# Moving two modulation units of the first scan chunk from its end into the place behind its first level update

## The chip, the cores and the metric

The kernel runs on one core of one Trainium2 chip. The metric is the device time of one execution in microseconds (us).

## The reference

Two layers of a diffusion trunk over 512 latent tokens and 256 context tokens, model width 1024, float32. Each layer modulates its input with shifts, scales and gates that come from a conditioning vector, then runs a mixer (latent attention, a bidirectional gated delta rule, pooling) and a mixture of experts. Two parts matter here.

The modulation is a matrix product of two vectors (one for latent, one for context tokens) with a matrix of 1024 by 6144 per layer:

```python
m = jnp.split(jax.nn.silu(c) @ ada_w[l] + ada_b[l], ADA_CHUNKS, axis=-1)
mc = jnp.split(jax.nn.silu(c_ctx) @ ada_w[l] + ada_b[l], ADA_CHUNKS, axis=-1)
```

The gated delta rule is a scan over chunks of tokens. Each chunk needs the inverse of a unit lower triangular matrix, and its state depends on that of the chunk before:

```python
w = lax.linalg.triangular_solve(tmat, kb * jnp.exp(gc)[..., None], ...)
u = lax.linalg.triangular_solve(tmat, vc * bc[..., None], ...)
def step(s, inp):
    v_new = u_i - jnp.einsum('bhcd,bhde->bhce', w_i, s)
    ...
```

## The kernel before, in words

The kernel is written as one program for each engine: PE (TensorE, matrix products), ACT (ScalarE), DVE (VectorE), POOL (GpSimd) and SP (SyncE, which issues the large loads). Each program is a fixed list in order; engines wait for each other on semaphores. Products go to 8 PSUM banks, handed out in rotation by `claim`: a bank can be claimed again only after its last product was read out, and the order of all claims in the PE program settles which bank a product gets.

**The scan** takes the 768 tokens in 6 chunks (`NT`), j = 0 to 5, for both directions and 4 heads at once. Within a chunk PE inverts the triangular block by levels: for each of two levels a `level_factor` (L1145), whose result DVE reads into `gW` (L2923), and a `level_update` (L1163), whose four results ACT copies back into the block (L2339). The next level's factor needs these copies. Then come the last level's product (`z6`, L1257), read out by ACT (L2344), and `u6` (L1269). A chunk has seven slots, 0 to 6, filled by `gdn_between`: slot 0 at its start, 1 behind the first factor, 2 behind the first update, 3 behind the second factor, 4 behind the second update, 5 behind z6, 6 behind u6. The table `BETWEEN` puts the state products of chunk j-1 into slots 0 to 3 and those that prepare chunk j+1 into slots 4 to 6. In chunk 0 slots 0 to 3 hold no state products. ACT's program has the same slots. In slots 3 and 5 of chunk 0 it also computes the decays of chunk 1 for one direction each (`next_decays`, L2209 to L2217), and there they stand behind the slot's modulation units. POOL multiplies these decays (`decays`, L3418), then copies the inverse of the chunk (L3534, L3535), and with that releases the first product of the next chunk (`v`, L1076) on PE.

**The modulation units.** The 48 column blocks of 256 columns of the modulation matrices are numbered; 0 to 7 are used at the start of the kernel, and from block `ADA_FIRST` = 8 on they are spread over the slots of the first layer's scan, 6 in a chunk, in the order of their numbers, as the table `ADA_SLOTS` says (its first row for chunk 0, its second for all others). One unit consists of:

- a load of 1 MB (`in_ada_w`) by SP (L1786) into one of 4 buffers of `ring`, `LENT` of them; SP issues these loads in order, each as soon as the last use of its buffer is done. Units 8 to 13 use buffers 3, 0, 1, 2, 3, 0. Buffer 2 holds tables of the scan at first, so the load of unit 11 also waits for POOL's `one_sided(0)` (L3427);
- 16 products on PE (`ada_load`, L717) into a claimed bank;
- on ACT (`ada_out`) a copy of the bank to one of two row buffers `arow` (L1940, profile name dT) and two small DMAs of 4 KB that write the rows to memory (L1949, `ada_rows`). As there are two row buffers, the copy of unit a first waits until the writes of unit a-2 have landed:

```python
if ADA_FIRST <= a - 2 < ADA_LATE:
    act.wait_ge(*ada_written(a - 2))
m = act.copy(arow[:, a % 2, :], b[:, 0:SLOT_COLS])
```

The write itself waits for the copy on the same engine, and everything behind it in ACT's list waits with it. The rows are read back at the end of the scan.

Of the kernel before, what the change touches and what calls it, by code (L numbers as in the profile page):

```python
# [92 lines left out]
    (("kr", 0), ("kr", 1), ("kk", 0)), (("ks", 0), ("ks", 1)), (("kk", 1), ("t0", 0), ("qk", 0), ("qk", 1)))  # L93
G_SLOTS = (3, 5)
GATES, SUMS, ROWS, LANES_EXP = (2, 1), (6, 3), (8, 4), (11, 7)
ADA_SLOTS = ((0, 1, 0, 1, 1, 1, 2), (1, 1, 1, 1, 1, 1, 0))


ADA_LOADS = 6 * D // 256
# [70 lines left out]
def build_program(nc, A, out):  # L170
    ctx = ExitStack()
    with ctx:
# [368 lines left out]
        def ada_at(j, slot):  # L541

            counts = ADA_SLOTS[min(j, 1)]
            first = ADA_FIRST + ADA_CHUNK * j + sum(counts[:slot])
# [3147 lines left out]
```

How the kernel before makes its waits and increments, by code:

```python
        def in_sum_made(eng, l, name, q):  # L305
            eng.wait_ge(sems[l]["lin"], sums_of(l) + 4 * q + int(name[1]))
# [1 line left out]
        def tokens_made(eng, l):  # L309
            eng.wait_ge(sems[l]["comb"], l * (1 + IN_PAIRS) + 1)
# [1 line left out]
        def taps_added(eng, l, q):  # L313
            eng.wait_ge(sems[l]["comb"], l * (1 + IN_PAIRS) + 2 + q)
# [5 lines left out]
        def lead_copied(eng, l, n):  # L321
            eng.wait_ge(sems[l]["lead"], l * (IN_PAIRS + OUT_PAIRS) + n + 1)
# [1 line left out]
        def sum_made(eng, l, name, p=0):  # L325
            eng.wait_ge(sems[l]["lin"], sums_of(l) + 4 * IN_PAIRS + OUT_SUMS[l].index((name, p)) + 1)
# [168 lines left out]
        def product_ready(eng, key, i=None):  # L496
            b, n, per = where[key]
            eng.wait_ge(bank_full[b], plus(n + 1, per, i))
            return psum[:, b, :]
# [5 lines left out]
        def evacuated(eng, key, i=None):  # L506
            b, n, per = where[key]
            eng.wait_ge(bank_free[b], plus(n + 1, per, i))
# [100 lines left out]
            def bank_unused(b):  # L610
                if b in second_of:
                    pe.wait_ge(bank_free[second_of[b][0]], second_of[b][1])
                elif uses[b]:
                    pe.wait_ge(bank_free[b], uses[b])
# [39 lines left out]
            def weights(name, n=None):  # L655
# [8 lines left out]
                        slot = len(loads) % (LENT if lends else SLOTS)  # L664
                    n = take_slot(name, slot)
                pe.wait_ge(slot_full[slot_of[n]], 16 * (nth_in[n] + 1))
                return ring[:, slot_of[n], :].rearrange("p (k c) -> p k c", k=KD)
```

## Time and profile before

| what | value |
| --- | --- |
| three runs | 1713.82 us median (1710.08 to 1714.26) |
| profiled execution: its own time | 1711.98 us |
| profiled execution: span of the trace | 1710.2 us |
| PE busy | 1622.6 us, 95% of the span |
| DVE, ACT, POOL busy | 734.0, 466.8, 570.6 us |
| scan of the first layer | about 359.6 to 510 us of the span |

Times in the rows are microseconds from the start of the span. "PE busy" counts products that overlap in the array, so that 95% isn't the array at its peak. "Idle before" with an arrow names what ended a wait; "issue" means that the profile shows nothing the engine waited for. Rows of the kind SPq and ACTq are the issue of a DMA, not its transfer. The granted TensorE clock (PEclk) is 1.00 at 2.4 GHz and 0.50 at 1.2 GHz.

### The profile page before, as it was taken

The numbers are of one execution on the slowest core, as the hardware profiler recorded it, in microseconds if no ns is written. First come the engines' busy times: TensorE is split into PE (matmuls) and PEld (weight loads), VectorE is DVE, ScalarE is ACT, GpSimd is POOL, SyncE is SP. The second block draws the span as 40 slices with busy tenths as digits, with TensorE's granted clock in tenths as the row PEclk, the third lists the DMA queues.
The fourth block names the chain that finished last, engine by engine and source line by source line (L and its number), as shares of the span: only waits on it lengthen the run. The fifth ranks groups of instructions, "written<-read, shape, count | busy, mean of one in ns | idle before, by whom it ended". The sixth has DMA issues, their size and how long they took to land. (4 is left out here: it accounts for less than half of the span.)

```text
span 1710.2 us, 36038 instructions
## 1 busy us (share of the span) xinstructions
PE 1622.6 (95%) x14725; PEld 1111.0 (65%) x14725; DVE 734.0 (43%) x1515; ACT 466.8 (27%) x1042; POOL 570.6 (33%) x698
## 2 busy tenths in 40 slices
PE   6999999889999999999999999999978999999998
PEld 4577776567878875555555447786568986554544
DVE  4357443345545351112111545744456675224233
ACT  4212433253333031121111231253363222111111
POOL 2756304226566203111110145611538881000000
PEclk9999999999999989999999999999989999999999
DMA  9320101059785158999998402010221035899995
GB/s 336 101 103 28 48 9 34 13 188 294 247 265 177 51 196 300 370 366 356 357 357 327 139 18 81 25 50 17 63 80 30 15 124 199 332 413 408 410 414 231
DMA packets 160357, 323.73 MB, mean 189 GB/s; under 512 B 30152, under 2 KB 118126, under 8 KB 144878
## 3 DMA queue, kind: packets, MB, share of 16 engines
q1 hardware_dynamic: 127584, 287.20, 45.7%
q0 software_dynamic: 7008, 21.74, 4.6%
q10 hardware_dynamic: 25646, 13.12, 2.7%
q8 instruction: 86, 1.41, 0.3%
q14 instruction: 33, 0.27, 0.0%
HBM read 307.31 MB, written 14.71 MB: 188 GB/s over the span
## 5 line engine op out<-in xcount | busy, mean ns | idle before, releaser
L1529 PE MATMUL psum<-ring,arena 128*64 128x256 f32 x1536 | 172.8, 381 | 7.1 <-DVE arena L3126 3.4
L1529 PEld LDWEIGHTS psum<-ring,arena 128*64 128x64 f32 x1536 | 108.6, 137 | 68.5 <-issue 17.1
L3637 POOL DMA_INDIRECT big<-h_rows_lat,idx x16 | 15.7, 984 | 347.3 <-PE psum L1662 174.0
L800 PE MATMUL psum<-hT,ring 128*128 128x256 f32 (+2 forms) x496 | 130.7, 423 | 0.0
L3147 DVE TENSOR_TENSOR arena<-arena,psum 128x384 f32<-128x384 f32 (+1 forms) x32 | 15.6, 488 | 259.0 <-PE psum L1538 159.9
L800 PEld LDWEIGHTS psum<-hT,ring 128*128 128x128 f32 (+1 forms) x496 | 93.3, 190 | 37.9 <-issue 27.4
L3185 DVE SCALAR_TENSOR_TENSOR xT<-psum,modraw,xT 128x512 f32<-128x512 f32 (+1 forms) x136 | 79.7, 622 | 48.5 <-PE psum L1616 33.8
L973 PE MATMUL psum<-hT,ring 128*128 128x256 f32 (+1 forms) x192 | 80.1, 526 | 0.0
L2439 ACT COPY arena<-psum 128x512 f32<-128x512 f32 (+2 forms) x49 | 23.7, 484 | 205.2 <-PE psum L1551 144.7
L1612 PE MATMUL psum<-arena 128*128 128x512 f32 x144 | 65.8, 602 | 4.4 <-DVE arena L3172 2.7
L2749 DVE TENSOR_REDUCE small<-psum 128x1 f32<-128x768 f32 (+1 forms) x40 | 33.9, 850 | 81.6 <-PE psum L994 81.5
L2443 ACT ACTIVATE arena<-psum 128x384 f32<-128x384 f32 (+1 forms) x32 | 14.0, 438 | 200.1 <-PE psum L1529 102.5
L994 PE MATMUL psum<-arena 96*128 96x256 f32 (+1 forms) x144 | 54.1, 496 | 10.1 <-ACT arena L2294 3.3
L1529 PE MATMUL psum<-big,arena 128*64 128x256 f32 x256 | 59.6, 381 | 0.0
L1557 PE MATMUL psum<-hT,arena 128*64 128x512 f32 x192 | 58.4, 598 | 0.0
L1557 PE MATMUL psum<-sz,arena 128*64 128x512 f32 x128 | 58.4, 598 | 0.0
L3126 DVE TENSOR_SCALAR arena<-psum,small 128x128 f32<-128x128 f32 x96 | 31.2, 383 | 62.9 <-PE psum L1664 55.5
L2430 ACT ACTIVATE arena<-psum,small 128x128 f32<-128x128 f32 x96 | 35.2, 441 | 71.4 <-PE psum L1664 45.4
L717 PE MATMUL psum<-ring,scol 128*32 128x256 f32 x768 | 52.5, 398 | 0.2 <-issue 0.2
L994 PEld LDWEIGHTS psum<-arena 96*128 96x128 f32 x144 | 25.2, 190 | 39.4 <-issue 28.2
L1612 PEld LDWEIGHTS psum<-arena 128*128 128x128 f32 x144 | 26.0, 189 | 36.7 <-issue 36.7
L1538 PE MATMUL psum<-ring,arena 128*32 128x128 f32 x1536 | 48.7, 275 | 0.0
(476 smaller groups left out, 3777.7 us busy)
## 6 DMA issues: line engine op xcount, KB each, us to landing
ring<-in_moe_w_gate SPq DMA_DIRECT2D x64, 1024.0 KB, 7.5
ring<-in_ada_w SPq DMA_DIRECT2D x48, 1024.0 KB, 6.6
ring<-in_moe_w_up SPq DMA_DIRECT2D x32, 1024.0 KB, 11.0
hT<-in_moe_w_down SPq DMA_DIRECT2D x24, 1024.0 KB
ring<-in_w_in SPq DMA_DIRECT2D x20, 1024.0 KB, 6.1
big<-in_moe_w_up SPq DMA_DIRECT2D x16, 1024.0 KB
sz<-in_moe_w_down SPq DMA_DIRECT2D x16, 1024.0 KB
big<-in_moe_w_down SPq DMA_DIRECT2D x16, 1024.0 KB
```

Source lines behind the costliest of these rows:

```text
L717: m = pe.matmul(ada[1][r:r + 32, 0:SLOT_COLS], lhsT=scol[:, 2 * k:2 * k + 32], rhs=ada[2][:, k, :], start=half == 0, stop=half == 1)
L800: m = pe.matmul(b[0:c1 - c0, 0:n], lhsT=w[:, k, c0:c1], rhs=hT[:, k, t0:t0 + n], start=k == 0, stop=k == KD - 1)
L973: x = pe.matmul(b[:, 0:n], lhsT=w[:, k, m % 2 * P:(m % 2 + 1) * P], rhs=hT[:, k, t0:t0 + n], start=k == 0, stop=k == KD - 1)
L994: m = pe.matmul(b[:, k0 * P:(k0 + nk) * P], lhsT=QT[0:QK, h, i * P:(i + 1) * P], rhs=KT[0:QK, h, k0 * P:(k0 + nk) * P], start=True, stop=True)
L1529: m = pe.matmul(b[e * CAP_L:(e + 1) * CAP_L, 0:2 * P], lhsT=xs[:, k, e, 0:CAP_L], rhs=w[e][:, 2 * (k - ks[0]) + q, :], start=k == 0, stop= ...
L1538: m = pe.matmul(b[r:r + CAP_C, 2 * P:3 * P], lhsT=xs[:, k, e, CAP_L:CAP], rhs=v[:, 2 * (k % (KD // 2)) + q, f * P:(f + 1) * P], start=k == ...
L1557: m = pe.matmul(ys[c][e * CAP_L:(e + 1) * CAP_L, :], lhsT=hidT[:, q, f * P + e * CAP_L:f * P + (e + 1) * CAP_L], rhs=w[e][:, f, c * 512:(c ...
L1612: m = pe.matmul(b[:, 0:SEQ], lhsT=ylat[:, k * P:(k + 1) * P], rhs=Sl[:, :], start=True, stop=True)
L2430: modulated_slots(lambda dst, x, k, c: act.activation(dst, x, ACT.Identity, bias=modp[:, 1, c, k:k + 1], scale=modp[:, 0, c, k:k + 1]), b, ...
L2749: dve.reduce_max(nm[:, n % 2:n % 2 + 1], scores_ready(dve, l, i, h), AX.X, negate=True).then_inc(s["nm"], 1)
L3126: modulated_slots(lambda dst, x, k, c: dve.tensor_scalar(dst, x, modp[:, 0, c, k:k + 1], modp[:, 1, c, k:k + 1], ALU.mult, ALU.add), b, xs ...
L3185: read_out(dve.scalar_tensor_tensor(out=x, in0=b[:, 0:n], scalar=mods_of[l][:, 5 * KD + k, 1 - g:2 - g], in1=x, op0=ALU.mult, op1=ALU.add) ...
```

## The change

The first row of the table says how many units stand in each slot of chunk 0. Before, units 8 to 13 stood in slots 1, 3, 4, 5, 6, 6. After, they stand in slots 1, 2, 2, 3, 4, 5. The same two tables are read by PE's and ACT's programs; SP's order of loads stays.

```diff
-ADA_SLOTS = ((0, 1, 0, 1, 1, 1, 2), (1, 1, 1, 1, 1, 1, 0))
+ADA_SLOTS = ((0, 1, 2, 1, 1, 1, 0), (1, 1, 1, 1, 1, 1, 0))
```

So units 9 and 10 are issued behind the first update, units 11, 12 and 13 take the slots that 9, 10 and 11 had, and slot 6 is empty.

## Rows read from the trace of the kernel before

**Rows 1.** Busy time by stretch, chunks 0, 1 and 3; last columns granted clock, DMA share, GB/s

```profile
359.60:385.70 26.10, 19.50 (x401) 14.28 (x401) 9.38 (x23) 15.76 (x38) 8.20 (x12) 0.87 0.88 275
385.70:412.00 26.30, 25.15 (x461) 20.07 (x462) 14.86 (x34) 10.20 (x32) 15.27 (x18) 1.00 1.03 330
440.00:467.00 27.00, 27.00 (x486) 22.19 (x485) 14.81 (x33) 10.21 (x32) 17.32 (x20) 1.00 0.83 264
```

**Rows 2.** Timeline of PE, chunk 0: start, duration, what, idle before

```profile
360.23 1.07 PE L717 MATMUL psum<-ring,scol 128*32 128x256 f32 x16
...
367.12 1.23 PE L1145 MATMUL psum<-ring,mlaw 64*64 64x64 f32 x32 [4.22 <-ACT ring L2339]
...
375.76 0.46 PE L1257 MATMUL psum<-ring 64*64 64x64 f32 x16 [0.66 <-ACT ring L2339]
...
377.18 1.07 PE L717 MATMUL psum<-ring,scol 128*32 128x256 f32 x16
...
382.49 1.93 PE L717 MATMUL psum<-ring,scol 128*32 128x256 f32 x32
385.71 2.02 PE L1076 MATMUL psum<-arena,ring 128*128 128x128 f32 x16 [1.29 <-issue]
```

**Rows 3.** Timeline of ACT, chunk 0

```profile
365.05 0.37 ACT L1940 COPY dT<-psum 128x256 f32<-128x256 f32 x1
365.45 1.11 ACTq L1949 DMA_DIRECT2D ada_rows<-dT  x2
366.61 1.20 ACT L2339 COPY ring<-psum 128x256 f32<-128x256 f32 x4 [1.18 <-issue]
370.28 0.37 ACT L1940 COPY dT<-psum 128x256 f32<-128x256 f32 x1 [2.48 <-PE psum L717]
...
371.74 1.28 ACT L2209 ACTIVATE arena<-arena,small 128x128 f32<-128x128 f32 x4 [1.08 <-issue]
...
378.31 0.37 ACT L1940 COPY dT<-psum 128x256 f32<-128x256 f32 x1 [0.88 <-PE psum L717]
...
379.77 1.28 ACT L2209 ACTIVATE arena<-arena,small 128x128 f32<-128x128 f32 x4 [1.08 <-issue]
```

**Rows 4.** Timeline of POOL, end of chunk 0

```profile
382.63 1.04 POOL L3418 TENSOR_TENSOR arena<-arena,small 128x512 f32<-128x512 f32 x1 [6.99 <-ACT small L2217]
...
385.21 0.40 POOL L3535 COPY ring<-ring 64x256 f32<-64x256 f32 x1
```

**Rows 5.** Timeline of ACT, from the end of chunk 0 into chunk 1

```profile
384.03 1.00 ACTq L1949 DMA_DIRECT2D ada_rows<-dT  x2
...
385.53 1.00 ACTq L1949 DMA_DIRECT2D ada_rows<-dT  x2
...
389.62 0.37 ACT L1940 COPY dT<-psum 128x256 f32<-128x256 f32 x1 [4.12 <-DMA ada_rows<-dT]
...
391.82 0.37 ACT L1940 COPY dT<-psum 128x256 f32<-128x256 f32 x1 [1.83 <-DMA ada_rows<-dT]
```

**Rows 6.** Timeline of SP's queue: issues of the loads of units 9 to 13

```profile
355.25 1.00 SPq L1786 DMA_DIRECT2D ring<-in_ada_w  x2
...
363.55 1.61 SPq L1786 DMA_DIRECT2D ring<-in_ada_w  x2
...
370.28 0.37 SPq L1786 DMA_DIRECT2D ring<-in_ada_w  x1
```

**Rows 7.** DMA: issue around 364; SP's queue (q1) 366.0 to 368.9; ACT's (q10) 368.9 to 371.5

```profile
ring<-in_ada_w SPq DMA_DIRECT2D x1, 1024.0 KB, 8.2
...
q1 hardware_dynamic: 1022, 1.03, 106.6%
...
q10 hardware_dynamic: 16, 0.01, 1.1%
```

**Rows 8.** Busy time by stretch: idle and half-clock stretch of PE in chunk 0

```profile
362.80:365.30 2.50, 0.10 (x7) 0.00 (x0) 0.00 (x0) 2.48 (x4) 2.24 (x5) 1.00 0.76 226
...
367.10:372.10 5.00, 4.98 (x113) 3.49 (x113) 0.75 (x2) 1.44 (x6) 0.00 (x0) 0.50 1.00 311
```

## The prediction

> **What bounds the kernel now.** I looked first at the busy time of the scan's chunks [rows 1]. A later chunk is PE from end to end (27.0 of 27.0 us), and chunk 1 nearly so (25.15 of 26.3). Chunk 0 isn't: it takes 26.1 us with 19.5 of PE. The change touches chunk 0 alone, so the question is what sets the end of that chunk, and whether PE-bound chunks behind it pass a shift on. They do: nothing in them has slack on PE to give a delay back.
>
> Next the timelines of PE, ACT and POOL in chunk 0, read backwards from the first product of chunk 1 at 385.71 [rows 2]. POOL's last copy of the chunk ends at 385.61, right ahead of it, and that run of copies stands behind POOL's decay product at 382.63, which waited 6.99 us for ACT's decays [rows 4]. These are ACT's second set, started at 379.77; ahead of it stands the unit in slot 5, copied at 378.31 after a wait of 0.88 us for its products, which PE had begun at 377.18 behind z6 [rows 2, 3]. z6, at 375.76, waited for ACT's copies of the second update. They stand in ACT's list behind the first set of decays, started at 371.74, and this behind the unit in slot 3, copied at 370.28 after ACT had been idle for 2.48 us [rows 3]. So from slot 3 on ACT's list is the chain: what delays the first set of decays delays the end of the chunk by the same. PE has room: 4.22 us idle behind the first update [rows 2], and its two units of slot 6 (382.49 to 384.42) end 1.29 us before it can go on, so they aren't on the chain.
>
> **The change, part by part.** PE issues the same 96 products in chunk 0. Nothing is gained by taking the pair out of slot 6: 1.93 us of PE that lay under the wait for POOL, at a price of nothing before and after. In slot 2 the pair falls into the 4.22 us of idle time, from about 362.9 to 365.0; the loads of units 9 and 10, issued from 355.25 to 356.25 [rows 6], were first in their queue, and I take them as landed. On PE the move is hidden.
>
> ACT does not lose its two units, it gets them earlier: before, units 8 to 11 stood ahead of the second set of decays, afterwards 8 to 13. One unit costs ACT a copy of 0.37 us and, as the write waits for the copy, about 1.1 us for its two issues: from 365.05 to 366.56 is 1.5 us [rows 3]. After the first update's copies (366.61 to 367.81) ACT would do units 9, 10 and 11 before the first decays, if nothing else held them: 367.85 + 3 x 1.45 = 372.2, against 371.74. The 2.48 us of idle time cover most of it: +0.5 us.
>
> But the copy of unit a waits for the writes of unit a-2, and that is what changes the sum. In the kernel before, this wait shows where two units stood close together, the pair of slot 6: their writes were issued at 384.03 and 385.53, and the copies that needed them ran at 389.62 and 391.82, the profile naming that DMA [rows 5]. From the first issue that is 5.6 and 6.3 us. The writes of unit 8, issued from 365.45 [rows 3], moved only between 368.9 and 371.5, after the 1 MB loads that had been issued at 363.55 and 363.96 [rows 6, 7]: 1.03 MB of SP's queue moved from 366.0 to 368.9 with no write between. These rows agree with writes that wait for the loads issued ahead of them.
>
> So in the changed kernel:
>
> - unit 9: copied at 367.85, writes issued 368.3 to 369.3;
> - unit 10: waits for the writes of unit 8, about 371.5, copy and issue to 373.0;
> - unit 11: waits for the writes of unit 9. By the two waits of rows 5 they land 5.6 to 6.3 us after 368.3, at 373.9 to 374.6. But more loads stand in front of them now: as PE frees buffers 0 and 1 in slot 2, the loads of units 13 and 14 go out from about 365; before, that of unit 13 went out at 370.28 [rows 6]. Units 11 to 14 are 4 MB. From the q1 row 1.03 MB take 2.9 us; starting at about 365.3 the four end near 368.3, 371.5, 374.6 and 377.7. If the writes of unit 9 wait for all of them they land at 378.0. Copy and issue of unit 11 take 1.45 us;
> - first decays: 375.4 to 376.1 in the one case, 379.5 in the other, against 371.74: +3.7 to +4.4, or +7.7 us.
>
> The products of unit 11 aren't late by this. Its load goes out at 363.55 as before, since it waits for POOL and not for a unit; the load behind it landed 8.2 us after 363.96 [rows 7], so at 372.2, and unit 11's one load earlier, near 369. PE waits a little for it in slot 3, but ACT wants it at 373 at the earliest. For the banks I counted claims: the eighth claim behind unit 10 is the first product of slot 4, and the one behind unit 11 is unit 12. These too become free at 372 and 375 to 378, ahead of z6, which waits for the copies behind the decays anyway.
>
> Then the clock. The stretch before the next z6 is one in which PE has nothing: unit 12 is done and z6 waits while ACT works off decays and copies, some 4 us (371.74 to 375.76 in the kernel before, where PE filled it with the late second update). Before, PE stood still from 362.8, and the granted clock was at 0.50 from about 365.3 to 372.1, 5.0 us of work long [rows 8]: half speed, 1.2 GHz. With the same fall ahead of z6, z6, the products behind it and unit 13, from 375.76 to 378.25 in the kernel before, 2.5 us, take up to twice as long, and ACT's last unit waits for them: +2.3 us. At the end of the chunk slot 6 is empty, and PE's gap grows from 1.29 to up to 3.2 us, less what half speed has made late; half a microsecond more for a fall there. What comes back: chunk 1 no longer has the two DMA waits of ACT, but PE hid nearly all of them. PE is idle for 1.15 us in all of chunk 1 [rows 1], so I give back 0.5, of at most 1.15.
>
> Sum: with all loads ahead of the writes 7.7 + 2.3 + 0.5 - 0.5 = +10.0 us; with the landing times of rows 5, 4.0 + 2.3 + 0.5 - 0.5 = +6.3 us. I take +8.5, nearer to the first because every write whose move I could see came after the loads issued before it. The profiled execution then comes to 1711.98 + 8.5 = 1720.5, and the median of runs, which lies 1.84 us above it, to 1722.3.
>
> The Trainium skill (DMA: Bandwidth & Descriptors, Queues, rings and completion order) says that each DMA engine takes turns between its queues packet by packet, so that a small write need not sit behind whole loads. By that rule the writes of unit 9 would land soon after their issue and the sum would be that of the first rival below. The trace does not agree: 16 packets of ACT's queue in 2.6 us, and none in the 2.9 us before [rows 7].
>
> **The rivals.** First, the writes don't wait: they land within 2.5 us, before unit 11 is due. Then the first decays start at 371.74 + 0.5 to + 1.4, PE has no long gap before z6, and only the emptied slot 6 can cost clock (0 to 2 us). Less the 0.5 of chunk 1: 0 to +3 us, no measurable change, 1713.8 to 1717. For it speaks that each write is 4 KB; against it rows 5 and 7. It decides at 371: a landing of unit 9's writes before that makes it.
>
> Second, the clock holds: no fall before z6, because PE's waits for banks in slots 3 and 4 break the idle time into parts. Then only the wait stays: +3.7 to +7.7, 1717.5 to 1721.5.
>
> Third, on the other side, the move shortens chunk 0: PE is at full clock behind the first update, since its idle time there falls from 4.22 to about 2 us, so that the second factor and update end earlier, and the pair's ACT work (2 x 1.45 us) no longer sits between the chunks, where ACT's waits of 4.12 and 1.83 us [rows 5] held the copies of chunk 1's first update. The gain is the 1.29 us gap at the boundary and the 1.15 us of PE idle time in chunk 1: -2.4 us, 1711.4. It needs writes landing before 369.3. Even all the idle time of chunk 0, 26.1 - 19.5 = 6.6 us, would be only 0.39%, so a gain above 0.3% wants nearly the whole of it; nothing points there, as ACT's chain has more ahead of it and not less.
>
> **How the numbers follow.** Writes behind loads, +6 to +10: 0.55. The same wait without the clock, +4 to +8: 0.18. Writes that don't wait, 0 to +3: 0.19. The boundary gains: 0.08. A measurement of this kernel can tell about 0.3%, 5.1 us, from no change. Of the first case 0.50 lies above that (0.05 below, where wait and clock are at their least), of the second 0.10. Slower 0.60; the same 0.36; faster 0.04, a half of the last case, for runs that spread over 4 us. Range: from the third rival's upper part, 1712.5, to the first sum with both falls of clock and a wait longer by a load, 1727.5.
>
> **What would show it.** In the trace of the changed kernel ACT's copies of units 10 and 11 are released by the DMA to `ada_rows`, near 371.5 and 374 to 378; the first decays start at 375.4 or later; z6 is at 379.5 to 383.5, behind an idle PE and at half clock; the first product of chunk 1 starts at 391 to 396 against 385.71, and all chunks behind it are shifted by that. ACT's DMA waits in chunk 1 are gone. Wrong is the forecast if L1940 shows no DMA wait in chunk 0, or if the loads of units 13 and 14 are not issued until the writes have gone.

## The result and the profile after

The changed kernel is slower, by less than was forecast: 1715.32 us median (1712.33 to 1720.86) against 1712.24 us (1708.17 to 1717.79), 22 runs each. The ratio is 1.0021, with a 95% interval of 1.0012 to 1.0030: 3.6 us, 2.1 to 5.1. The forecast was +8.5 us, a range of 1712.5 to 1727.5, and slower by over 0.3% with a chance of 0.60. The measured value lies below 0.3%, inside the range, and is less than half of the forecast loss. The profiled execution has a span of 1713.0 us, 2.8 more than before.

The start of the scan moves from execution to execution for reasons that lie ahead of the edit: the first factor of chunk 0 starts at 359.61 us before and at 358.32 after, and between 358.32 and 363.68 over the 14 traces of this study. So all places of the scan are given below as time from that first factor.

The timeline of ACT in chunk 0 of the changed kernel; it answers to [rows 3]:

```profile
363.75 0.37 ACT L1940 COPY dT<-psum 128x256 f32<-128x256 f32 x1
364.16 1.11 ACTq L1949 DMA_DIRECT2D ada_rows<-dT  x2
365.31 1.20 ACT L2339 COPY ring<-psum 128x256 f32<-128x256 f32 x4 [1.18 <-issue]
366.37 0.41 ACT L1940 COPY dT<-psum 128x256 f32<-128x256 f32 x1
366.82 1.00 ACTq L1949 DMA_DIRECT2D ada_rows<-dT  x2
370.42 0.37 ACT L1940 COPY dT<-psum 128x256 f32<-128x256 f32 x1 [3.63 <-DMA ada_rows<-dT]
...
372.31 0.37 ACT L1940 COPY dT<-psum 128x256 f32<-128x256 f32 x1 [1.52 <-DMA ada_rows<-dT]
...
373.76 1.28 ACT L2209 ACTIVATE arena<-arena,small 128x128 f32<-128x128 f32 x4 [1.08 <-issue]
...
381.91 0.37 ACT L1940 COPY dT<-psum 128x256 f32<-128x256 f32 x1 [2.45 <-PE psum L717]
...
383.37 1.28 ACT L2209 ACTIVATE arena<-arena,small 128x128 f32<-128x128 f32 x4 [1.09 <-issue]
```

The copies of units 10 and 11 (370.42 and 372.31) end waits that the profile puts down to the writes of the rows. The first decays stand behind them: 373.76, which is 15.44 from the first factor, against 12.13 before. In [rows 3] the same place shows a wait for PE, and none for a DMA.

The timeline of PE in the same stretch, for [rows 2]:

```profile
358.32 0.69 PE L1145 MATMUL psum<-ring,mlaw 64*64 64x64 f32 x32
...
363.68 1.07 PE L717 MATMUL psum<-ring,scol 128*32 128x256 f32 x16 [1.07 <-DMA ring<-in_ada_w]
365.83 1.08 PE L1145 MATMUL psum<-ring,mlaw 64*64 64x64 f32 x32 [1.08 <-ACT ring L2339]
367.83 1.94 PE L717 MATMUL psum<-ring,scol 128*32 128x256 f32 x16 [0.92 <-DMA ring<-in_ada_w]
...
377.78 0.48 PE L1257 MATMUL psum<-ring 64*64 64x64 f32 x16 [3.31 <-ACT ring L2339]
...
380.09 1.74 PE L717 MATMUL psum<-ring,scol 128*32 128x256 f32 x16
...
389.30 3.75 PE L1076 MATMUL psum<-arena,ring 128*128 128x128 f32 x16 [3.16 <-issue]
392.98 1.94 PE L717 MATMUL psum<-ring,scol 128*32 128x256 f32 x16
394.85 0.81 PE L1145 MATMUL psum<-ring,mlaw 64*64 64x64 f32 x32
```

The pair sits in the old gap as intended: PE now waits 1.07 us for a load and 1.08 for ACT where it waited 4.22. But z6 waits 3.31 us for ACT where it waited 0.66, and the chunk ends with a gap of 3.16 us in place of 1.29. The second factor starts 7.51 us from the first in both kernels. The busy times of the two gaps and of what follows them have the granted clock in the third column from the right:

```profile
374.50:377.80 3.30, 0.02 (x3) 0.05 (x3) 0.05 (x1) 3.24 (x11) 1.04 (x1) 1.00 1.10 351
377.80:381.80 4.00, 4.00 (x42) 2.51 (x42) 3.16 (x8) 0.56 (x3) 0.00 (x0) 0.57 1.14 333
386.10:389.30 3.20, 0.04 (x1) 0.03 (x1) 1.86 (x6) 0.06 (x1) 2.62 (x5) 0.85 0.11 38
389.30:394.90 5.60, 5.60 (x36) 4.11 (x36) 3.37 (x7) 0.00 (x0) 5.25 (x7) 0.50 0.01 3
```

Behind each gap PE works at half speed: 0.57 on average over the 4 us behind the first, 0.50 for the whole of the first 5.6 us of chunk 1. The products that open chunk 1 take 3.75 us, where [rows 2] have 2.02.

One thing the pair did not change: the clock falls behind the first update here too, though no single wait of PE is longer than 1.08 us there. From 362.6 to 367.9 PE is busy for 2.23 of 5.30 us, and then:

```profile
367.90:371.10 3.20, 3.20 (x68) 2.03 (x72) 0.00 (x0) 0.37 (x1) 0.00 (x0) 0.50 1.08 363
```

In the kernel before, the clock was at 0.50 over the same products of the second update [rows 8].

The places of both kernels and of all experiments, each the start in its PE or ACT timeline less the start of its first factor. The last column is the first product of the output projection behind the scan (L1330).

| kernel | first decays | z6 | chunk 1, first product | chunk 1, first factor | chunk 2, first product | projection |
| --- | --- | --- | --- | --- | --- | --- |
| before | 12.13 | 16.15 | 26.10 | 29.05 | 52.76 | 164.75 |
| before, second trace | 12.12 | 16.14 | 26.07 | 29.03 | 53.37 | 164.49 |
| changed | 15.44 | 19.46 | 30.98 | 36.53 | 58.95 | 170.53 |
| changed, second trace | 15.43 | 19.44 | 30.72 | 35.21 | 57.49 | 168.14 |
| changed, third trace | 15.58 | 19.60 | 30.86 | 35.37 | 57.32 | 168.33 |
| changed, decays first | 13.19 | 18.67 | 26.35 | 29.30 | 51.42 | 161.90 |
| changed, end gap filled | 15.77 | 19.79 | 32.22 | 35.09 | 57.29 | 168.36 |
| changed, gap at z6 filled | 15.70 | 21.96 | 31.90 | 34.86 | 57.79 | 168.43 |
| changed, both gaps filled | 16.05 | 20.07 | 30.00 | 32.95 | 55.61 | 165.86 |
| changed, three row buffers | 13.06 | 17.09 | 27.02 | 32.57 | 56.38 | 168.02 |
| changed, loads held | 12.89 | 17.07 | 27.60 | 30.55 | 52.48 | 163.53 |
| before, decays first | 8.05 | 15.33 | 23.92 | 26.90 | 53.00 | 163.47 |
| before, one unit moved | 14.05 | 18.07 | 28.02 | 30.97 | 52.90 | 164.47 |
| changed, three buffers and decays first | 11.01 | 16.49 | 23.99 | 26.95 | 49.34 | 160.30 |

Within one kernel these places repeat to 0.3 us up to the first product of chunk 1, much better than whole runs do.

### The profile page after: what moved, and what is told of

It is laid out like the page before. It is cut to its first block and busy times, and to the rows that moved or that the text cites. A ratio compares the mean times of both kernels' runs of the same rounds, so it can differ in the third digit from the quotient of the medians.

```text
span 1713.0 us, 36038 instructions
## 1 busy us (share of the span) xinstructions
PE 1621.4 (95%) x14725; PEld 1110.2 (65%) x14725; DVE 734.6 (43%) x1515; ACT 466.2 (27%) x1042; POOL 570.6 (33%) x698
## 5 line engine op out<-in xcount | busy, mean ns | idle before, releaser
L2439 ACT COPY arena<-psum 128x512 f32<-128x512 f32 (+2 forms) x49 | 23.7, 484 | 204.7 <-PE psum L1551 145.0
```

## The experiments

Two theories stood against each other after the result. By the first, the wait of a copy for the writes of the unit two before it delays ACT's list, and the clock falls in the gaps that this opens. By the rivals, PE's own late products (its loads), or ACT's longer list as such, or something at the chunk's end would do it.

**The decays ahead of the unit.** In ACT's program alone:

```diff
+ if j == 0 and slot in G_SLOTS:
+     next_decays(1, G_SLOTS.index(slot))
  for a in ada_at(j, slot) if l == 0 else ():
      ada_out(a)
- if j == 0 and slot in G_SLOTS:
-     next_decays(1, G_SLOTS.index(slot))
```

> The changed kernel, but in chunk 0 ACT does the decays of chunk 1 ahead of the modulation unit in slots 3 and 5, and not behind it. Times are counted from the first factor of chunk 0. If the wait for the row writes is what delays the decays, the first decays start about 9 to 10 us in (16.7 in the changed kernel, 12.1 in the one before) unless unit 10's copy, which still stands ahead of them in slot 2, holds them: then about 13.6, right behind that copy. z6 starts at 16 to 18 us (19.5 changed, 16.2 before) and the first product of chunk 1 at 24 to 27 us (31.0 changed, 26.1 before): 4 to 7 us less than the changed kernel. If PE's late products, for its own loads, set the chunk, the reordering of ACT's list changes less than 1 us.

Measured: the ratio to the kernel before is 0.9997 (0.9986 to 1.0008), so the loss is gone. ACT's timeline:

```profile
375.41 0.37 ACT L1940 COPY dT<-psum 128x256 f32<-128x256 f32 x1 [3.27 <-DMA ada_rows<-dT]
375.81 1.00 ACTq L1949 DMA_DIRECT2D ada_rows<-dT  x2
376.87 1.28 ACT L2209 ACTIVATE arena<-arena,small 128x128 f32<-128x128 f32 x4 [1.08 <-issue]
```

Unit 10's wait is still there and still ahead of the decays; unit 11's is not. (The 16.7 us that the expectation names for the changed kernel is not the start of its first decays; that is 15.4.) z6 came at 18.67, above the 16 to 18 expected. It waited 1.30 us for ACT's copies of the second update, which still stand behind the decays and unit 11 in ACT's list; before that PE had waited 1.23 us for the copy of unit 11 to free a bank. The first product of chunk 1 is at 26.35, 4.6 us earlier than in the changed kernel. PE's work and its loads were as in the changed kernel, so the order of ACT's list is what carries the delay.

**Filling the end gap.** Products that nobody reads, in slot 6 of chunk 0:

```diff
+ if j == 0 and slot == 6:
+     stay_warm(5)
```

> The changed kernel, with 5 products whose result nobody reads at the emptied slot 6, some 3 us of PE work in the 3.2 us gap at the end of chunk 0. If the gap lets the clock fall and the first products of chunk 1 run at half speed for it, the clock holds at 1.00, these products take 2.0 us and not 3.75, and the first factor of chunk 1 starts about 2.6 us earlier than in the changed kernel (33.9 against 36.5 us from the first factor of chunk 0). If the late factor has another cause (masks, reads of the banks), it stays at 36.5 or moves later by what the added work overruns.

Measured: ratio 1.0045 (1.0031 to 1.0059). The five products took 4.46 us and not 3, so chunk 1 began 1.24 us later than in the changed kernel. Even so its first factor came 1.44 us earlier (35.09 against 36.53; against the second and third trace of the changed kernel, 35.21 and 35.37, it is only 0.1 and 0.3 us). What shows the clock is the opening products, which took 1.95 us, not 3.75, and the 2.87 us from the first product to the first factor, not 5.55. PE's timeline:

```profile
389.79 4.46 PE L677 MATMUL psum<-lev 128*128 128x512 f32 x10
394.09 1.95 PE L1076 MATMUL psum<-arena,ring 128*128 128x128 f32 x16
```

The loss of whole runs, 0.45%, is larger than that of the changed kernel, though the projection is no later (168.36). What the difference is made of isn't shown.

**Filling the gap ahead of z6.** Thirteen products nobody reads, within unit 12:

```diff
+ if a == 12:
+     for _ in range(13):
+         m = pe.matmul(ada[1][:, 256:512], lhsT=lev[:, 0, 0:2, :], rhs=lev[:, 0:2, 0:2, :], start=True, stop=True)
```

> The changed kernel, with 13 products whose result nobody reads in unit 12 (slot 4), some 2.8 us of PE work in the 3.3 us gap before z6. If the clock falls in that gap, it now holds: z6, the products behind it and unit 13 take 2.5 us and not 4.0, ACT's copy of unit 13 starts 1.5 us earlier against z6, and so does the first product of chunk 1 (29.4 against 31.0 us from the first factor). z6 itself stays where it is (19.5), as it waits for ACT. If the clock has no part in it, the first product of chunk 1 stays at 31.0.

Measured: ratio 1.0016 (0.9999 to 1.0034). The filling took 5.88 us, twice what was meant, and held z6 back by 2.5 us. From z6 to the first product of chunk 1 it is 9.94 us, as before the change (9.95), against 11.52 in the changed kernel (11.28 and 11.26 in its other traces). That is the 1.3 to 1.6 us of the clock ahead of z6.

**Three row buffers.** Units 8 to 19 rotate through three buffers (the third is an idle part of another tile), and a copy waits for the last user of its own:

```diff
+ row_bufs = [arow[:, 0, :], arow[:, 1, :], mlaw[:, 2 * G1:2 * G1 + SLOT_COLS]]
+ row_of = [(a - ADA_FIRST) % 3 if a < ADA_FIRST + 12 else a % 2 for a in range(ADA_FIRST, ADA_LATE)]
...
- if ADA_FIRST <= a - 2 < ADA_LATE:
-     act.wait_ge(*ada_written(a - 2))
+ for x in row_before(a, r) if a < ADA_LATE + 2 else ():
+     act.wait_ge(*ada_written(x))
```

> The changed kernel with three row buffers for units 8 to 19, so that the copy of a unit waits for the writes of the unit three before it, not two. Unit 10's copy then waits for nothing and unit 11's for the writes of unit 8, which landed 12.1 us from the first factor in the changed kernel. If the wait for the writes is the cause, the first decays start at 13.6 to 14 us (15.4 changed, 12.1 before) and the first product of chunk 1 comes 1.5 to 3.5 us earlier than in the changed kernel. If the writes only pass the time in which ACT would wait for something else, nothing moves by more than 0.5 us.

Measured: ratio 0.9998 (0.9981 to 1.0014). ACT's and PE's timelines:

```profile
372.92 0.37 ACT L1947 COPY dT<-psum 128x256 f32<-128x256 f32 x1 [1.66 <-DMA ada_rows<-dT]
...
374.38 1.28 ACT L2218 ACTIVATE arena<-arena,small 128x128 f32<-128x128 f32 x4 [1.08 <-issue]
```

```profile
378.41 0.46 PE L1262 MATMUL psum<-ring 64*64 64x64 f32 x16 [1.09 <-ACT ring L2348]
...
388.34 3.75 PE L1081 MATMUL psum<-arena,ring 128*128 128x128 f32 x16 [3.14 <-issue]
```

Unit 10 does not wait for a write, unit 11 does for 1.66 us. The decays come 2.4 us earlier than in the changed kernel and chunk 1 4.0 us, both more than expected; z6 waits only 1.09 us, and no clock is lost behind it (z6 to chunk 1: 9.93 us). At the end of the chunk the gap is as long as before, 3.14 us, and the clock is lost there, 3.75 us again. So the two losses of clock are separate, and the first hangs on the wait.

**The decays first, on the kernel before.** The same edit as in the first experiment.

> The kernel before, with ACT's decays ahead of the unit in slots 3 and 5 of chunk 0, the edit of the first experiment alone. If ACT's list from slot 3 on is the chain of chunk 0 in this kernel too, the first decays start 8.3 us from the first factor and not 12.1, z6 at 14 to 15.5 (16.2 before) and the first product of chunk 1 at 22.5 to 25 (26.1 before): the edit alone makes the kernel before 1 to 3.5 us faster. If it gives nothing here, the first experiment's gain over the changed kernel was the undoing of the wait for the writes alone, and the first product of chunk 1 stays at 25.5 to 26.5.

Measured: ratio 0.9990 (0.9975 to 1.0004). The places up to chunk 1 came as expected: decays at 8.05, z6 at 15.33, chunk 1 at 23.92, 2.2 us earlier than before. At the projection 1.0 to 1.3 us of it are left, and the whole time can't be told from no change. ACT's list was the chain of chunk 0 before the change, too.

**One unit moved.** The table's first row as (0, 1, 1, 1, 1, 1, 1).

> The kernel before with one unit moved, not two: units 8 to 13 in slots 1, 2, 3, 4, 5, 6. Now one unit more stands ahead of ACT's first decays, unit 10, and its copy waits for the writes of unit 8. By the wait for writes these land about 12.1 us from the first factor, the decays start at 13.6 (12.1 before, 15.4 changed), z6 at 17.6, and the first product of chunk 1 at 27.5, plus 1.5 where the clock falls ahead of z6: half the loss of the change. If only the pair in one slot did the harm, by its 3 us of ACT work and PE's wait for loads, one unit costs nothing and that product stays at 26.1.

Measured: ratio 1.0006 (0.9993 to 1.0019). ACT's timeline:

```profile
374.79 0.37 ACT L1940 COPY dT<-psum 128x256 f32<-128x256 f32 x1 [4.12 <-DMA ada_rows<-dT]
375.19 1.00 ACTq L1949 DMA_DIRECT2D ada_rows<-dT  x2
376.24 1.28 ACT L2209 ACTIVATE arena<-arena,small 128x128 f32<-128x128 f32 x4 [1.08 <-issue]
```

One unit is enough to bring the wait in: decays at 14.05, first product of chunk 1 at 28.02, 1.9 us late and 0.5 later than expected. PE's gaps ahead of z6 and at the chunk's end were 2.27 and 2.15 us, and no clock was lost behind either. By the projection nothing is left of this delay (164.47).

**Three buffers and the decays first**, the two edits together on the changed kernel.

> The changed kernel with both remedies: three row buffers, and the decays ahead of the unit in slots 3 and 5. Unit 10's copy then waits for nothing, and nothing that waits stands ahead of the first decays: they start at 11.2 us from the first factor, against 13.2 with the decays first alone. z6 at 15.5 to 16.5, first product of chunk 1 at 23.5 to 25 (26.35 with the decays first alone, 26.1 before). If it is not the writes that hold unit 10, that product stays at 26.3.

Measured: 1709.63 against 1711.70 us, ratio 0.9983 (0.9968 to 0.9998). Every place came as expected: decays 11.01, z6 16.49, chunk 1 at 23.99, 7.0 us earlier than in the changed kernel. Chunk 1 keeps its pace, and the projection is 4.2 to 4.5 us earlier than before. It is the only version here whose interval lies below 1.

**The loads held.** SP waits with the load of unit 12, and all behind it, until the writes of unit 9 have landed:

```diff
+ if m == 12:
+     sp.wait_ge(*ada_written(9))
```

> The changed kernel, but SP issues the load of unit 12, and all behind it, only when the writes of unit 9 have landed. So only unit 11's load is under way beside the writes of units 8 and 9. If the writes take 5.5 to 6.3 us because loads of 1 MB share the 16 DMA engines with them, they now land within 2 to 3.5 us of their issue, unit 10's and 11's copies wait at most 0.5 us, and the first decays start at 12 to 13.3 us from the first factor (15.4 changed). If the time of a write is its own, the waits stay at 3.6 and 1.5 us. Unit 12's products come later in either case, ahead of z6 or just behind.

Measured: ratio 0.9999 (0.9986 to 1.0012). ACT's timeline:

```profile
364.74 1.11 ACTq L1951 DMA_DIRECT2D ada_rows<-dT  x2
...
368.50 0.37 ACT L1942 COPY dT<-psum 128x256 f32<-128x256 f32 x1 [1.13 <-DMA ada_rows<-dT]
...
370.35 0.37 ACT L1942 COPY dT<-psum 128x256 f32<-128x256 f32 x1 [1.48 <-PE psum L717]
...
371.80 1.28 ACT L2211 ACTIVATE arena<-arena,small 128x128 f32<-128x128 f32 x4 [1.08 <-issue]
```

Unit 8's writes land 3.8 us after their issue and not 6.3; unit 11's copy waits for its products (1.48 us) and no longer for unit 9's writes. The landing of unit 8's writes and the wait of 1.13 us are above the 2 to 3.5 and the 0.5 expected: one load was still under way beside them. PE now waits for loads (1.10 us for unit 12's, 0.54 for 13's), and yet chunk 1 begins 3.4 us earlier than in the changed kernel. The end gap, 3.13 us, cost no clock here:

```profile
383.40:386.50 3.10, 0.00 (x0) 0.02 (x1) 1.85 (x6) 0.00 (x0) 2.62 (x5) 1.00 1.10 350
386.50:389.40 2.90, 2.89 (x32) 2.26 (x32) 2.90 (x7) 0.00 (x0) 2.54 (x4) 1.00 1.12 351
```

**Both gaps filled to size**, 7 products in unit 12 and 3 in slot 6.

> The changed kernel with both of PE's gaps in chunk 0 filled to size: 7 products nobody reads in unit 12, 3.2 us, and 3 at slot 6, 2.7 us. Only the wait for the writes is left of the loss. If the account of wait and clock is right, z6 stays at 19.5 us from the first factor, the first product of chunk 1 is at 29.4 (31.0 changed, 26.1 before) and the first factor of chunk 1 at 32.4 (36.5 changed, 29.05 before): 3.3 us behind the kernel before at both places. If the clock isn't what costs there, they stay near 31.0 and 36.5.

Measured: 9.93 us from z6 to chunk 1 and 2.95 from there to the first factor, as before the change; the places themselves are 0.6 us later than expected, since the wait of unit 10 was 4.61 us in this execution:

```profile
381.88 0.46 PE L1263 MATMUL psum<-ring 64*64 64x64 f32 x16 [0.28 <-ACT ring L2345]
...
388.51 2.74 PE L677 MATMUL psum<-lev 128*128 128x512 f32 x6
391.81 2.02 PE L1080 MATMUL psum<-arena,ring 128*128 128x128 f32 x16 [0.56 <-issue]
```

Its first factor of chunk 1 is 2.3 to 3.6 us earlier than in the traces of the changed kernel. The whole time does not show it: ratio 1.0031 (1.0012 to 1.0049), a loss of 2.1 to 8.4 us, where the projection is 1.1 to 1.4 us later than in the kernel before. In its trace, what follows the first factor takes 1351.3 us, against 1350.6 and 1353.7 in the two traces of the kernel before. So the places and the runs disagree here, and I can't say what the difference is made of.

**The two kernels again**, for their traces.

> The changed kernel once more, for its trace. The waits for the writes are there again within 0.7 us (first decays 14.7 to 16.2 us from the first factor), as nothing random stands behind them. The clock may fall or hold: where the fall ahead of z6 or at the end of chunk 0 is a matter of the execution, z6 to the first product of chunk 1 is either 9.9 or 11.5 us, and from there to the first factor either 3.0 or 5.6. If both come out as in the first trace, 11.5 and 5.6, the falls belong to the kernel.

> As for the run ahead of it: a third trace of the changed kernel. Waits as in the first within 0.7 us, the clock's part free to differ. If the clock is a matter of the execution, at least one of the two new traces has 9.9 in place of 11.5 or 3.0 in place of 5.6.

> The kernel before once more, for its trace. Its gap behind the first update is 4.2 us, so the clock falls there again and the first decays start 12.1 us from the first factor within 0.4; the first product of chunk 1 at 26.1 within 0.4, the first factor of chunk 1 at 29.05 within 0.4. If these places vary by more, the two traces of the change can't be compared to a microsecond.

Measured: the decays are within 0.15 us of the first trace in the changed kernel and within 0.01 in the kernel before, so the wait belongs to the kernel. z6 to chunk 1 takes 11.28 and 11.26 us (11.52 in the first trace), chunk 1's first product to its first factor 4.49 and 4.51 (5.55). Neither came back to 9.9 or 3.0: the clock falls in both gaps in all three traces, but how much it costs behind the end gap differs by 1.1 us. PE's timeline of the second trace:

```profile
392.42 3.57 PE L1076 MATMUL psum<-arena,ring 128*128 128x128 f32 x16 [2.92 <-issue]
395.91 1.07 PE L717 MATMUL psum<-ring,scol 128*32 128x256 f32 x16
```

## Why the prediction was right in kind and wrong in size

**PE's gap takes the pair, and slot 6 was off the chain.** Right. The second factor starts at the same place, 7.51 us from the first. Not foreseen was PE's wait of 1.07 us for the load of unit 10, which the prediction took as landed; the 0.92 us for that of unit 11 it had named. They cost nothing, since the second factor waits for ACT after the first of them and ACT takes unit 11 only later; with the loads held PE waits for four of them, and chunk 1 still begins earlier.

**ACT's list is the chain, and unit 10 waits for unit 8's writes.** Right, to 0.2 us: the forecast 371.5 is 11.9 from the first factor, and the copy ran at 12.1. Three experiments that shorten these waits or take the decays out from behind one (decays first, three buffers, loads held) take chunk 1 from 31.0 to 26.4, 27.0 and 27.6.

**Unit 9's writes: the step that failed.** The prediction worked out 373.9 to 374.6 from [rows 5] and 378.0 for writes that wait for every load issued before them, and took a value nearer to the second: its +8.5 us holds 6.2 us for this term (8.5 less 2.3 for the clock; the two terms of 0.5 cancel). The decays measured 3.3. The copy of unit 11 ran at 13.99, which is 373.6 on the scale of the kernel before, 0.3 us below the near end. So the first decays (375.05 on that scale), z6 (379.1) and the first product of chunk 1 (390.6) all came just below the places that the prediction gave for them. The writes of unit 9, issued at 366.82, landed 5.5 us later, at 372.3. The load of unit 13 had been issued ahead of them, at 364.19, and landed only at 375.7:

```profile
ring<-in_ada_w SPq DMA_DIRECT2D x1, 1024.0 KB, 11.5
```

The load behind it, issued from 364.86, took 13.9 us. So a write does not wait for all loads issued before it. It does not go at once either: the load of unit 12, issued at 362.68, took 8.5 us and landed at 371.2, ahead of unit 9's writes.

The rows of the kernel before showed this already, and the prediction misread them. By its own 8.2 us the load issued at 363.96 landed at 372.2, which is after the 371.5 by which the writes of unit 8 had moved. In the 2.6 us in which the 16 packets of ACT's queue moved [rows 7], SP's queue moved on as well:

```profile
q1 hardware_dynamic: 816, 0.82, 96.6%
```

So these rows don't speak against engines that take turns between queues, though the prediction says that they do. What they do show is the time ahead of that, in which none of the writes' packets moved. The upper case was also added up too high: at 1.03 MB in 2.9 us, 4 MB from 365.3 end near 377.1 and not 377.7. And the top of the range, 1727.5, is 0.6 us more than its terms give (1713.8 + 10.0 + 3.1). That the loads under way do matter is shown by holding them: 3.8 us in place of 6.3.

**The clock ahead of z6.** Right in place, forecast +2.3, measured 1.3 to 1.6 us over three traces; gone in both kernels that fill the gap (9.94 and 9.93 us from z6 to chunk 1), and in two that shorten it (three buffers 9.93, one unit moved 9.95).

**The clock at the end of chunk 0.** Under-sized: forecast +0.5, measured 1.5, 1.6 and 2.6. I had let the late PE work of the first fall eat up the second gap; it was 2.9 to 3.2 us long all the same, since POOL's part of the chain moved with ACT's.

**What comes back.** Under-sized, and this is the largest miss beside unit 9. The prediction gave back 0.5 us, of at most 1.15, that being PE's idle time in chunk 1 [rows 1], and held that PE-bound chunks pass a shift on. From the first factor of chunk 1 to the projection the kernel before takes 135.7 and 135.5 us, the changed one 134.0, 132.9 and 133.0: it recovers 1.5 to 2.8 us, being late by 6.2 to 7.5 us at the first place and by 3.4 to 6.0 at the second. Most of that comes in chunk 1. From its first factor to the first product of chunk 2 the kernel before takes 23.7 and 24.3 us, of which PE is idle for 1.1 and 1.6; in all three traces of the changed kernel PE is not idle there at all, and the stretch takes 22.4, 22.3 and 22.0. Before (the first row) and changed:

```profile
388.66:412.37 23.71, 22.57 (x437) 18.18 (x434) 12.27 (x29) 10.20 (x32) 12.78 (x16) 1.00 1.03 325
394.85:417.27 22.42, 22.42 (x436) 18.26 (x433) 12.05 (x28) 10.21 (x32) 10.19 (x14) 0.99 0.94 302
```

So all of the idle time came back and not half of it, and a little PE time with it. The long form goes with the pair in slot 6: the kernel before with the decays first, which has the pair and ACT's DMA waits in chunk 1, takes 26.1 us, the other kernels of the table 21.9 to 22.9, and 23.8 with three buffers. That ACT's waits cause it wasn't tried apart. From chunk 2 to the projection the kernels differ by no more than their own traces do. The same recovery is why one unit moved costs 1.9 us at chunk 1 and nothing at the projection.

**The sum** with the measured terms, as means over the traces: 3.3 + 1.4 + 1.9 - 2.3 = +4.3 us, at the projection, where the three traces of the changed kernel show 3.4 to 6.0. Against the forecast of +8.5, the wait is 2.9 less, what comes back 1.8 more and the clock ahead of z6 0.9 less; the 1.4 us that the clock at the chunk's end was put too low hid a part of this, which was luck.

Behind the projection more comes back. Near 580 us the products of the router and those behind them (L1395 to L1344) run partly at half speed, on the same work in every kernel: in the two first traces the clock was at 0.50 for 6.5 us before and for some 3.5 after. They take 10.4 us in both traces of the kernel before and 8.7 in all three of the changed one, so behind them the changed kernel is late by 1.7 to 4.4 us, 2.7 on average; whole runs say +3.6 (2.1 to 5.1). Over all 14 traces this stretch takes 10.4 us in five, 8.7 in seven and 7.05 in two. What decides between them isn't shown.

Of the rivals, the one in which writes don't wait is refuted by the two DMA waits, though the measured +3.6 us lies nearer to its 0 to +3 than to the forecast: the size alone would have spoken for the wrong mechanism. The clock that holds is refuted by all three traces. The gain at the boundary did not come, and its premise of a full clock behind the first update did not hold either; but the version with the wait and the order mended has it, and more: it was ACT's list, not PE's gap, that had to be shortened. Up to chunk 1 its gain is that of the order alone (23.99 against 23.92 in the kernel before with the decays first); behind that it is 3.7 us ahead of this one by chunk 2, with slot 6 empty.

## What to carry to other kernels

Moving work into an idle gap of one engine also moves what it hangs on the other engines' lists: here PE had 4 us to give, and ACT had the chain. Before placing such a unit, ask what its copy waits for, how far away the same buffer was last used, and what stands behind it in that engine's list; put the work that the chain needs ahead of anything that may wait for a DMA. A shift in one chunk can't be added to the whole time unreduced: check with a place far behind the edit how much of it survives.

## What the runs showed of the hardware

- Two writes of 4 KB, issued while 1 MB loads are under way, took 5.4 to 7.3 us to land, and 3.8 with one load under way (loads held). The Trainium skill (DMA: Bandwidth & Descriptors, Queues, rings and completion order) has the DMA engines take turns between queues packet by packet; the landing ahead of a load issued earlier agrees with that (372.3 against 375.7), the 5.5 us don't follow from it. The same section says that the semaphore increment of a DMA lands only behind all earlier writes of its DMA engine; that may be part of it, and no run here takes the two apart.
- With three loads outstanding, the issue of the next one held SP's queue for 3.38 us in place of 0.37 (3.46 and 2.90 in the other two traces of the changed kernel):

```profile
364.86 3.38 SPq L1786 DMA_DIRECT2D ring<-in_ada_w  x1
```

- A gap of PE of 2.9 to 3.2 us at the same place of the list was followed by half speed in four traces (the three of the changed kernel, three buffers) and by full speed in two (gap at z6 filled, loads held). How much a gap costs can't be read from its length. Nor does it take one long gap: behind the first update of the changed kernel, half speed followed three waits of 0.92 to 1.08 us within 5.3 us.
